# Eight of fourteen mixer projection units by seven products, the residual parked in DRAM, and a gate step reordered

## The reference

```
x = x + 0.5*swiglu(rmsnorm(x, norm_ffn1), ffn1_w_in, ffn1_w_out)      # D_FF = 2816
m, k, v, logf, s = token_mix(rmsnorm(x, norm_mix), w_in_mix, ...)     # HGRN2 heads and forgetting attention
x = x + m
x = x + 0.5*swiglu(rmsnorm(x, norm_ffn2), ffn2_w_in, ffn2_w_out)
y = rmsnorm(x, norm_final)

def token_mix(h, w_in, ...):
    p = h @ w_in        # q, f, i, g of HGRN2 (512 columns each), q, k, v of attention (512 each), 8 forget columns
    ...                 # recurrence, attention over the prompt and over 8 x 2048 cached rows
    out = concat(o_hgrn, o_fox) @ w_out
```

## Time and profile before

| | us |
|---|---|
| median of 3 runs | 1251.35 (1249.91 to 1252.42) |
| the profiled execution, its own time | 1252.58 |
| its span | 1250.7 |
| PE busy | 1210.6 (97%) |
| DVE busy | 819.7 (66%) |
| ACT busy | 572.0 (46%) |

### The profile page before, as it was taken

How to read it: one execution, slowest core, us unless ns; L and a number is a source line. 1 busy time by engine, 2 the same in 40 slices (tenths; PEclk the granted TensorE clock), 3 DMA queues, 4 the chain that set the end, 5 groups by cost and what they waited for, 6 DMA issues and landing times.

```text
span 1250.7 us, 29938 instructions
## 1 busy us (share of the span) xinstructions
PE 1210.6 (97%) x12005; PEld 1129.6 (90%) x12005; DVE 819.7 (66%) x1557; ACT 572.0 (46%) x1047; POOL 106.0 (8%) x247
## 2 busy tenths in 40 slices
PE   9999999999999999998978999999999999999998
PEld 8999999999999999996656666599989999999998
DVE  6799848838956423336756566654679839847954
ACT  6454424514534211535866776743345424524534
POOL 1000000000005000000222522214000000000000
PEclk9999999999999999999989999999999999999999
DMA  8133333233324343344798999723123332333322
GB/s 208 39 96 102 110 93 102 85 101 85 94 93 129 107 135 92 107 170 154 245 366 301 347 353 343 241 69 95 58 84 102 92 111 80 93 99 102 93 77 72
DMA packets 187145, 172.79 MB, mean 138 GB/s; under 512 B 11890, under 2 KB 149651, under 8 KB 187027
## 3 DMA queue, kind: packets, MB, share of 16 engines
q1 hardware_dynamic: 185858, 167.47, 42.5%
q0 software_dynamic: 1104, 3.67, 0.8%
q10 hardware_dynamic: 64, 0.02, 0.0%
HBM read 162.19 MB, written 8.93 MB: 137 GB/s over the span
## 4 chain that ended last, share of the span: by engine, by line
PE 82%; DVE 9%; issue 3%; ACT 3%; DMA 2%; SPq 0%; ACTq 0%; DVEq 0%; POOLq 0%
PE ps L2221 40%; PE ps L2359 28%; PE ps L1038 2%; PE ps L1123 2%; PE ps L1138 2%; PE ps L963 1%; DVE z_lo L2849 1%; PE ps L1003 1%; DMA d_keys<-in_cache_k 1%; PE ps L983 1%; DVE b_lo L2818 1%; PE ps L801 1%; ACT d_keysT L1383 1%; DVE z_sum L2826 0%; DMA d_log_f<-in_cache_logf,page_ids 0%
## 5 line engine op out<-in xcount | busy, mean ns | idle before, releaser
L2359 PE MATMUL ps<-b_lo,z_hi 128*128 128x272 f32 x1008 | 292.1, 290 | 0.0
L2359 PE MATMUL ps<-b_hi,z_hi 128*128 128x272 f32 x1008 | 290.8, 288 | 1.0 <-ACT z_kept L2566 1.0
L2359 PE MATMUL ps<-b_hi,z_lo 128*128 128x272 f32 x1008 | 290.9, 289 | 0.0
L2491 ACT ACTIVATE w_hi<-w_raw 128x2048 fp32r<-128x2048 f32 (+2 forms) x56 | 90.0, 1608 | 234.2 <-PE ps L2221 234.2
L2359 PEld LDWEIGHTS ps<-b_hi,z_hi 128*128 128x128 f32 x1008 | 190.0, 188 | 1.4 <-issue 1.4
L2359 PEld LDWEIGHTS ps<-b_hi,z_lo 128*128 128x128 f32 x1008 | 189.7, 188 | 0.0
L2359 PEld LDWEIGHTS ps<-b_lo,z_hi 128*128 128x128 f32 x1008 | 189.3, 188 | 0.0
L2221 PE MATMUL ps<-g_hi,w_hi 128*128 128x272 f32 x704 | 148.6, 290 | 6.6 <-DVE g_lo L2794 3.5
L2221 PE MATMUL ps<-n_hi,w_hi 128*128 128x272 f32 x704 | 148.9, 289 | 1.9 <-issue 1.0
L2221 PE MATMUL ps<-n_hi,w_lo 128*128 128x272 f32 x704 | 148.3, 288 | 0.0
L2221 PE MATMUL ps<-g_hi,w_lo 128*128 128x272 f32 x704 | 148.2, 289 | 0.0
(11 more groups left out here) (398 smaller groups left out, 1952.1 us busy)
## 6 DMA issues: line engine op xcount, KB each, us to landing
w_raw<-in_ffn_w_in SPq DMA_DIRECT2D x87, 512.0 KB, 5.0
d_keys<-in_cache_k SPq DMA_DIRECT2D x128, 256.0 KB, 5.3
d_values<-in_cache_v SPq DMA_DIRECT2D x124, 256.0 KB, 6.2
w_raw<-in_ffn_w_out SPq DMA_DIRECT2D x48, 384.0 KB, 3.6
w_raw<-in_w_in_mix SPq DMA_DIRECT2D x28, 512.0 KB, 4.8
w_raw<-in_ffn_w_out SPq DMA_DIRECT2D x16, 256.0 KB, 2.9
w_raw<-in_w_out_mix SPq DMA_DIRECT2D x8, 512.0 KB, 4.7
suffix_scratch<-d_log_f_sums SPq DMA_DIRECT2D x32, 64.0 KB, 2.1
```

What stands on the lines that cost most here:

```text
L2359: mm = pe.matmul(bank(out), w[j][:, a, k * P:(k + 1) * P], x, start=(k == 0 and n_pass == 0 and not more), stop=(k == KB - 1 and n_pass == ...
L2491: nc.scalar.activation(w_hi[j][:, 0:kt * UC], w_raw[j][:, 0:kt * UC], ACT.Copy).then_inc(w_hi_ready, 1)
```

## The change

1. U0 to U3 stay normal, with columns q of HGRN2 and q of attention. Eight units (here Z0 to Z7: k of attention, then f, i, g) take the seven-product form. The last pair (v of attention) is a normal pair whose moving operands are B11, B12, B21, B22, so B12's high and low parts are made in between. Results of these ten units need no `rstd`, which is in the operands.
2. Four of the seven high operands lie where `xT` was. `xT` is stored to a DRAM scratch (2.23 MB) by a DMA on SP between the two loads for U2 and U3, and loaded back after the first two suffix loads of the attention.
3. The tiles of the projection get another order in memory; value loads now wait for the end of Z7; `suffix_vector` comes after the operands' sums; sigmoid and silu move.
4. In chunk 0 of both FFNs, two of the four `build_full` instructions come behind the last `gate_step`, and so does the `split_lo` of O1. Output units take k = kt-2 for both tiles, then k = kt-1, each with a wait of its own.

```
@@ unit, ffn, gate_step, the mixer
-                    order = [(t, k) for ks in (range(kt - 2), range(kt - 2, kt)) for t in range(2) for k in ks]
+                    order = [(t, k) for ks in (range(kt - 2), (kt - 2,), (kt - 1,)) for t in range(2) for k in ks]
...
-                        if k == 0 or k == kt - 2:
-                            pe.wait_ge(g_ready, done - 2 if k == 0 else done)
+                        if k == 0 or k >= kt - 2:
+                            pe.wait_ge(g_ready, done - 2 if k == 0 else done - (kt - 1 - k))
...
-                split_lo(pair + 1, j, next_kt)
+                if not late_split:
+                    split_lo(pair + 1, j, next_kt)
...
                 nc.vector.tensor_tensor(lo, g_f[:, :, :], hi.bitcast(F32), ALU.subtract).then_inc(g_ready, 1)
+                if late_split:
+                    split_lo(pair + 1, j, next_kt)
...
-                        build_full(f, norm, range(KB, KD))
-                        gate_step(p0 + 1, 1, q0 + 3, f, 3, kt)
+                        build_full(s, norm, range(KB, KB + 2))
+                        gate_step(p0 + 1, 1, q0 + 3, f, 3, kt, late_split=True)
+                        build_full(s, norm, range(KB + 2, KD))
...
+                    if i == 1 and j == 0:
+                        sp.wait_ge(x_ready, KD)
+                        sp.dma_start(x_d, xT[:, :, :]).then_inc(x_landed[0], 16)
...
-            first_pair(P_MIX_IN, 1, n_hi[0], n_lo[0])
-            with pe.Fori(1, MIX_PAIRS) as i:
-                for j in range(2):
-                    unit(i + P_MIX_IN, j, KD, n_hi[0], n_lo[0])
+            first_pair(P_MIX_IN, 1, m_hi, m_lo)
+            for j in range(2):
+                unit(P_MIX_IN + 1, j, KD, m_hi, m_lo)
+            for n in range(MIX_ZN):
+                seven_products(MIX_FIRST + n, n % 2, MIX_Z + n, n, MIX)
+            pe.wait_ge(z_step, 5 * (MIX_Z + MIX_ZN) - 1)
+            for j in range(2):
+                normal_unit(2 * (P_MIX_OUT - 1) + j, j)
...
+            def normal_unit(unit_n, j):
+                pe.wait_ge(w_hi_ready, unit_n + 1)
+                pe.wait_ge(w_lo_ready, unit_n + 1)
+                pe.wait_ge(drained, unit_n - 1)
+                pe.wait_ge(x0_lo, B_FROM[MIX] + NW + 1)
@@ block.scalar, behind the loop over the eight units
+            first_tile_half(MIX_FIRST + MIX_ZN - 1, mix_rows(MIX_ZN - 1))
+            nc.scalar.activation(b_hi(MIX, B12), b_12[:, :, :], ACT.Copy).then_inc(x0_hi, 1)
+            split_hi(P_MIX_OUT - 1, 1, KD)
@@ block.vector, behind the loop over the eight units
+            mix_drained(MIX_Z + MIX_ZN - 1)
+            dve.wait_ge(x0_hi, B_FROM[MIX] + NW + 1)
+            nc.vector.tensor_tensor(b_lo(MIX, B12), b_12[:, :, :], b_hi(MIX, B12).bitcast(F32), ALU.subtract)\
+                .then_inc(x0_lo, 1)
+            split_lo(P_MIX_OUT - 1, 1, KD)
```

More of the change, by code:

```diff
@@ L2159, in _ @@
             ffn_loads(P_FFN[0], io["ffn1_w_in"], io["ffn1_w_out"], True)
-            for i, group in enumerate(MIX_PAIR_GROUP):
+            for i, rows in enumerate(MIX_ORDER):
+                group = MIX_COLUMNS[rows]
                 if i == 3:
@@ L2433, in _, with normal_columns @@
             ffn(0, P_FFN[0], 0)
-            first_pair(P_MIX_IN, 1, n_hi[0], n_lo[0])
-            with pe.Fori(1, MIX_PAIRS) as i:
-                for j in range(2):
-                    unit(i + P_MIX_IN, j, KD, n_hi[0], n_lo[0])
+            def normal_columns(k, half):
+                n = ((B11, B12), (B21, B22))[k // KB][half]
+                return b_hi(MIX, n)[:, k % KB, :], b_lo(MIX, n)[:, k % KB, :]
+            def normal_unit(unit_n, j):
[3 more added lines that the diff above has]
+                pe.wait_ge(x0_lo, B_FROM[MIX] + NW + 1)
+                for t in range(2):
+                    for k in range(KD):
+                        w = [m[j][:, k * UC + t * P:k * UC + (t + 1) * P] for m in (w_hi, w_lo)]
+                        for n, (wp, low) in enumerate(((w[0], 0), (w[0], 1), (w[1], 0))):
+                            for half in range(2):
+                                mm = pe.matmul(bank(4 * j + 2 * t + half), wp, normal_columns(k, half)[low],
+                                               start=(k == 0 and n == 0), stop=(k == KD - 1 and n == 2))
+                mm.then_inc(mm_done, 1)
+            first_pair(P_MIX_IN, 1, m_hi, m_lo)
[6 more added lines that the diff above has]
+                normal_unit(2 * (P_MIX_OUT - 1) + j, j)
             pe.wait_ge(wf_split, 2)
@@ L2801, in build_full @@
                     if d < KB:
-                        for half, out in enumerate((b_full(f, B11)[:, k, :], b_12[:, k, :])):
+                        for half, out in enumerate((b_full(s, B11)[:, k, :], b_12[:, k, :])):
                             nc.vector.scalar_tensor_tensor(out, xT[:, d, half * HALF:(half + 1) * HALF], gain,
@@ L3048, in project_out, with mix_drained, copy_out @@
+            def mix_drained(z):
+                dve.wait_ge(z_silu, 2 * z + 2)
+                dve.wait_ge(z_step, 5 * z + 5)
+                dve.sem_inc(drained, 1)
+            def copy_out(pair, j, tile):
+                dve.wait_ge(mm_done, 2 * pair + j + 1)
+                for t in range(2):
+                    op = nc.vector.tensor_copy(halves(pT[:, tile + t, :]), unit_psum(j, t))
+                op.then_inc(drained, 1)
             def project_out(pair, j, tile):
@@ L3059, in _ @@
                     mean_squares(2)
-                project_out(P_MIX_IN, j, 2 * j)
+                project_out(P_MIX_IN, j, MIX_ORDER[0] + 2 * j)
                 split_lo(P_MIX_IN + 1, j, KD)
+                build_full(MIX, 1, (range(KB), range(KB, KD))[j])
+            build_sum(MIX, U1, b_full(MIX, B11), b_12[:, :, :], ALU.subtract)
+            build_sum(MIX, T3, b_full(MIX, B22), b_12[:, :, :], ALU.subtract)
+            build_sum(MIX, T2, b_full(MIX, U1), b_full(MIX, B22), ALU.add)
             suffix_vector(dve)
-            with dve.Fori(1, MIX_PAIRS - 1) as i:
-                for j in range(2):
-                    project_out(i + P_MIX_IN, j, i * 4 + 2 * j)
-                    split_lo(i + (P_MIX_IN + 1), j, KD)
```

266 lines of the change are left out of this document (189 added, 77 removed).

## The result

The changed kernel takes 1255.84 us (median of 22 runs, 1249.93 to 1263.01), the kernel before 1251.92 beside it (22 runs). The ratio is 1.0032, 95% interval [1.0016, 1.0048]: slower by 0.32%. The forecast was 1251.6, "no change"; the measurement lies in its range of 1245.3 to 1257.5, outside the main case's own (1248.5 to 1254.5), and among the outcomes over 0.2% slower, to which the prediction gave 0.22. The profiled execution took 1257.44 us, its span 1255.5.

What follows compares the result with a forecast made beforehand. The prediction took PE's matmul stream (82% of the chain) plus its waits as the bound. Terms -11.4 + 0.7 + 3.35 + 1.4 + 1.8 + 1.6 + 1.35 + 1.6 = +0.4 us gave 1251.6 us, range 1245.3 to 1257.5.

Steps and rivals of the forecast that it cites:

- main case: Whole kernel: all terms as summed, +0.4 us, 1251.6 us, no change; own range 1248.5 to 1254.5, chance 0.53.
- Part 1: Eight mixer units in seven-product form: 10.59 instead of 12.02 us each, all on PE's path, -11.4 us.
- Part 2: Way into the seven-product units: DVE hand-overs and ACT's PSUM copies for Z1 slightly late, +0.7 us, between 0 and 4.
- rival D: Way into the seven-product units late by more, x store at its slow end: +3 us, 1254.6 us; chance 0.10.
- Part 3: Way out, ahead of U12: PE idle while B12's parts are made after Z7, +3.35 us, and low clock behind, +1.4.
- Part 4: Reordered gate step: g_lo waits go, O2 starts later, FFN 2 +1.8 us, FFN 1 +1.35, low clock +1.6 each.
- rival B: Behind the new PE gaps: the clock stays up, as behind 2.03 us; -4.6 from the sum, 1247.0 us; chance 0.17.
- Part 5: Reload of x at the start of the attention turns: fits where DMA is empty, 0; at worst +5.8 us.

Runs made afterwards that it cites:

- the undone reorder: The changed kernel with the reordered gate step taken back in both FFNs, the mixer's seven products kept: 1247.9 us, ratio 0.9968 to the kernel before.
- VectorE's new order: The changed kernel, reordered gate step kept, with VectorE's b_full pieces, sums and low parts around it put in another order: 1248.0 us, ratio 0.9962 to the kernel before.
- the double reload: The changed kernel with x read back from DRAM twice, SyncE's queue waiting for the first transfer: 1264.13 us, ratio 1.0105 to the kernel before.

## Why the prediction came out as it did

The profiled execution was forecast at 1253.0 and took 1257.44. By its own steps:

**Part 1, -11.4.** Right. VectorE's first weight sum of each seven-product unit, kernel after, shows the pitch, 10.59 and 10.62:

```profile
494.14 1.23 DVE L2923 TENSOR_TENSOR z_sum<-w_raw 128x1024 f32<-128x1024 f32 x1 [1.15 <-PE ps L2388]
...
504.73 1.23 DVE L2923 TENSOR_TENSOR z_sum<-w_raw 128x1024 f32<-128x1024 f32 x1 [1.14 <-PE ps L2388]
...
515.35 1.23 DVE L2923 TENSOR_TENSOR z_sum<-w_raw 128x1024 f32<-128x1024 f32 x1 [1.18 <-PE ps L2388]
```

**Part 2, +0.7.** Right in place and size for this execution: 0.66 us for ACT's PSUM copy behind Z2's weights. It is not steady, though: 1.80, 2.18, 1.64, 1.59, 0.72 and 1.25 us in the six other traces with the same code there, with a fall of the clock behind the 2.18. So 0.7 was in part luck. The store of x took 8.1 us to land (5.8 reckoned) and PE waited for nothing of it, so rival D is out. The 388 GB/s that the estimate took as the fullest window is not the fullest: the window from 620 us of the kernel before is at 418.

**Part 3, +3.35 and +1.4.** The gap was 2.96, the clock's fall cost 1.55. Over Parts 1 to 3 the forecast is -5.95. The trace has PE 6.45 us late at the end of U3, the last normal unit before the seven products (ScalarE's first instruction behind it starts at 450.49, before at 444.04), and VectorE's release of the attention 0.94 late (576.21 against 575.27), so -5.5; the undone reorder's time gives -4.0, interval [-6.1, -2.0].

**Part 4.** The failed step, in size only. The mechanism is as written: no wait for `g_lo`, O2's low weights last, and VectorE's given-up cover named as the reason. The gaps are right (FFN 1 1.75 against 1.35, FFN 2 1.96 against 1.8). The clock term was mis-sized: where 1.6 was forecast for FFN 2, the fall lasted twice as long as the others and cost 2.7. Together 6.35 was forecast for the part; the runs put it at 7.8, the trace at 8.0 (1.75 + 1.96 + 1.6 + 2.7).

**The term that is missing.** The 2.03 us gap of the earlier trace rows had been read as fixed. It ends a chain that begins with a gather, whose landing moves by 2 us between executions. In the changed kernel's profile it cost 1.7 us more, and 1.5 for the clock behind it. The prediction used that same gap as its case of a clock that stays up, and one execution was too little for that. At this place the clock fell behind gaps of 2.19, 2.30, 2.76, 3.65 and 3.72 us, and stayed up behind 1.65, 1.96, 2.03 and 2.90.

The terms add up to the miss. Against the forecast of 1253.0, Parts 1 to 3 gained 0.45 less, Part 4 cost 1.65 more, the missing term 3.2 and the attention 0.7 less: 4.6, where 4.4 was measured.

The chances erred the same way: rival B (the clock stays up) got 0.17 and the trace shows four falls in four gaps. The Trainium skill's rule (TensorE: Matmul & The Clock Gate, "Why this matters for your kernels"), that idle gaps between bursts bring half the clock back, was weighed and taken at part of its price. This trace agrees with it: each of the three new gaps had its fall. With the upper ends that the prediction itself names (1.7, 2.5 and 2.5 us), the sum would have been 2.1 us higher and nearer.

**Part 5, 0.** Right for one reload; the cover, 4.5 us of queue time, is smaller than the 15 us that the text made of it. Part of the misses is balanced by the attention, which took 0.7 us less: the clock was low there once for 6.8 us instead of three times for 3.4, which no step of the change explains.

What stays open: the changed kernel's own runs spread over 13 us (1249.93 to 1263.01). Most of that spread is the clock: over the 22 executions the mean granted clock goes from 0.984 to 0.994, and the time follows it (correlation -0.87, some 10 us for 0.01). The kernel before, in the 23 executions of the first group, has 0.994 in the mean, the changed kernel 0.988. Which gaps the clock answers in an execution, and why, stays open: the traces suggest that it is drawn anew each time, but only one execution of each kernel was recorded.

## What to carry over

A wait that is taken away from TensorE is won only if the instruction next in line on the feeding engine is early. Before moving an operation on a queue, look at the idle time it was hidden in: here 1.4 us of `build_full` left a 4.67 us idle stretch and went onto the path, and the opposite move, filling that stretch, won 8.8 us. Before a wait's clock behaviour is priced, look at more than one execution: the same gap went either way here. An operand that is built behind a loop should be tied to the last reader of its slot, not to the loop's end (4.9 us).

## What had not been expected of the hardware

- The clock's answer to a gap isn't a function of its length. The same 2.96 us gap ahead of U12 was followed by 0.50 in two traces (the changed kernel and the reorder undone) and by 1.00 in two others (VectorE's new order and the double reload). Ahead of O2 of FFN 1, 2.64 us went by at 1.00, while 2.38 and 2.55 us brought 0.50 in two other runs. Gaps of 1.88 to 1.90 us in FFN 1 brought 0.50 in three traces; 1.96, 2.03 and 2.90 us at the end of FFN 1 did not. These are the two stretches behind a gap of 2.96 us at full clock, first VectorE's new order, then the double reload; compare the window from 540 of the changed kernel:

```profile
537.32 0.48 PE L2479 MATMUL ps<-b_hi_x,w_hi 128*128 128x272 f32 x2 [2.96 <-DVE b_lo L3246]
```

```profile
537.00:539.00 2.00, 1.68 (x13) 1.71 (x14) 1.49 (x2) 1.97 (x3) 0.00 (x0) 1.00 0.94 305
539.00:541.00 2.00, 2.00 (x18) 2.00 (x17) 2.00 (x4) 2.00 (x4) 0.00 (x0) 1.00 0.99 330
```

```profile
537.27 0.49 PE L2481 MATMUL ps<-b_hi_x,w_hi 128*128 128x272 f32 x2 [2.96 <-DVE b_lo L3244]
```

```profile
539.27:541.27 2.00, 2.00 (x18) 2.00 (x18) 2.00 (x5) 1.98 (x5) 0.00 (x0) 1.00 0.89 297
```

- A fall can last twice as long: 6 us of TensorE's work at low clock behind the 4.95 us gap of FFN 2, 3.4 us behind the 5.14 us gap of FFN 1. That too is not set by the gap: 3.4 us behind the same gap of FFN 2 (4.94 us) in the run with the double reload.
- Reading 2.23 MB back took 10.1 us beside four key loads, and 9.8 and 9.3 us with no load behind it; the write took 8.1 us. All are slower than the 5.8 us that the prediction took from a window at 388 GB/s.
